# Tile-by-tile scaling at the norms of a two-block network, x ahead of the context in the odd norm, and the queries' rotation moved ahead of retention's gate projection

## What is computed

```python
def half_ffn(x, g, w1, w3, w2):
    return x + FFN_RES * swiglu(rmsnorm(x, g), w1, w3, w2)

def first_block(...):
    for layer in range(DEPTH):
        x = half_ffn(x, ...)
        h = rmsnorm(x, mix_norm[layer])
        x = x + (mixer_gla_rglru(h, ...) if layer % 2 == 0 else mixer_hgrn2(h, ...))
        x = half_ffn(x, ...)
        gate = jax.nn.sigmoid(rmsnorm(x, ple_norm[layer]) @ ple_gate[layer])
        x = x + gate * (p[layer] @ ple_proj[layer])
    return rmsnorm(x, final_norm)

def odd_layer(h, hc, w_in, w_out, q_norm, w_uq, kv_norm, w_ukv, decay_logit, need_ctx):
    cq, ckv, kr, rq, rk, rv, rg = split_cols(h @ w_in, widths)
    qn, qr, kn, vm = mla_up(cq, ckv)          # queries, keys, values from normed latents
    m = softmax_attention(qn, kn and knc, vm and vmc,
                          apply_axial_rope(qr, ang_r, ang_c), k_rope_all)
    r, r_c = retention_bidir(rq, rk, rv, ...)
    r = rms_norm(r) * jax.nn.silu(rg)
    return jnp.concatenate([m, r], axis=-1) @ w_out
```

## Time and profile before

| | before |
|---|---|
| median of 3 runs, us | 2898.67 |
| lowest and highest, us | 2896.55, 2899.17 |
| the profiled execution, us | 2900.66 |
| its span in the trace, us | 2898.5 |
| mean granted TensorE clock, share of full | 0.961 |
| TensorE matmul busy, share of the span | 90% |
| VectorE, ScalarE busy | 21%, 15% |

### The profile page before, as it was taken

How to read it: one execution, slowest core, us unless ns; L and a number is a source line. 1 busy time by engine, 2 the same in 40 slices (tenths; PEclk the granted TensorE clock), 3 DMA queues, 4 the chain that set the end, 5 groups by cost and what they waited for, 6 DMA issues and landing times.

```text
span 2898.5 us, 29860 instructions
## 1 busy us (share of the span) xinstructions
PE 2613.8 (90%) x12493; PEld 1816.4 (63%) x12493; DVE 618.5 (21%) x1323; ACT 442.3 (15%) x764; POOL 43.8 (2%) x55
## 2 busy tenths in 40 slices
PE   8999999999999999999999999898889998655656
PEld 7887788888888878888876563333334755211213
DVE  2011311022102241113134641211113143000002
ACT  1001310013002320003223520000002132000001
POOL 0000000000000011000000100000000000000000
PEclk9999999999999999999999999999999999788878
DMA  9446674455447487444422148999997216999997
GB/s 307 145 159 234 214 265 146 159 201 181 155 149 245 158 249 180 145 145 151 142 88 82 67 158 359 421 421 422 422 422 265 102 44 258 422 421 422 422 422 303
DMA packets 278241, 700.92 MB, mean 242 GB/s; under 512 B 16696, under 2 KB 200168, under 8 KB 230952
## 3 DMA queue, kind: packets, MB, share of 16 engines
q1 hardware_dynamic: 271088, 686.99, 63.8%
q10 hardware_dynamic: 4944, 8.07, 0.9%
q0 software_dynamic: 2112, 4.46, 0.8%
HBM read 695.30 MB, written 4.06 MB: 241 GB/s over the span
## 4 chain that ended last, share of the span: by engine, by line
PE 74%; DMA 19%; DVE 3%; issue 1%; SPq 1%; ACT 1%; ACTq 0%; DVEq 0%
PE bank L539 73%; DMA ring<-moe_w 19%; PE bank L548 2%; SPq L2952 1%; DVE AR L1571 0%; DVE AR L1574 0%; DVE AR L1583 0%; ACT AR L2386 0%; DVE H L1574 0%; DVE XC L1577 0%; DMA cst<-const 0%; DVE AR L1963 0%; ACT L2386 0%; DMA AR<-vec 0%; DVE H L1577 0%
## 5 line engine op out<-in xcount | busy, mean ns | idle before, releaser
L539 PE MATMUL bank<-H,ring 128*128 128x256 f32 (+1 forms) x5120 | 1149.2, 385 | 19.7 <-ACT H L2386 8.1
L539 PEld LDWEIGHTS bank<-H,ring 128*128 128x128 f32 (+1 forms) x5120 | 968.3, 190 | 188.5 <-issue 48.6
L539 PE MATMUL bank<-ring,AR 128*32 128x512 f32 (+1 forms) x2832 | 549.2, 703 | 204.0 <-DMA ring<-moe_w 196.7
L539 PEld LDWEIGHTS bank<-ring,AR 128*32 128x32 f32 (+1 forms) x2832 | 175.7, 140 | 559.6 <-issue 546.1
L539 PE MATMUL bank<-AR,ring 128*128 128x256 f32 (+2 forms) x1504 | 333.6, 380 | 5.1 <-DVE AR L1583 5.1
L539 PE MATMUL bank<-AR 128*128 128x256 f32 (+14 forms) x1200 | 307.0, 427 | 13.8 <-DVE AR L2289 6.2
L539 PEld LDWEIGHTS bank<-AR,ring 128*128 128x128 f32 (+2 forms) x1504 | 283.8, 189 | 47.9 <-DVE AR L1583 5.6
L2386 ACT ACTIVATE AR<-bank 128x512 f32<-128x512 f32 (+3 forms) x195 | 114.6, 590 | 1224.4 <-PE bank L539 816.2
L1571 DVE TENSOR_TENSOR AR<-bank,AR 128x512 f32<-128x512 f32 (+2 forms) x105 | 72.3, 689 | 832.2 <-PE bank L539 791.6
L539 PEld LDWEIGHTS bank<-AR 128*128 128x128 f32 (+7 forms) x1200 | 167.1, 181 | 113.5 <-issue 85.2
L2386 ACT ACTIVATE AR<-AR 128x512 f32<-128x512 f32 (+6 forms) x160 | 97.6, 635 | 866.9 <-DVE AR L1571 789.4
(11 more groups left out here) (124 smaller groups left out, 652.2 us busy)
## 6 DMA issues: line engine op xcount, KB each, us to landing
ring<-moe_w SPq DMA_DIRECT2D x368, 1024.0 KB, 15.5
ring<-ffn_w SPq DMA_DIRECT2D x132, 1024.0 KB, 5.2
ring<-ada_w SPq DMA_DIRECT2D x48, 1024.0 KB, 5.2
ring<-m_w_in SPq DMA_DIRECT2D x26, 1024.0 KB, 10.0
ring<-even_w_in SPq DMA_DIRECT2D x24, 1024.0 KB, 5.1
AR<-moe_w SPq DMA_DIRECT2D x18, 512.0 KB, 7.2
ring<-m_w_out SPq DMA_DIRECT2D x8, 1024.0 KB, 11.7
ring<-ple_gate SPq DMA_DIRECT2D x8, 1024.0 KB, 5.1
```

The source lines that it names most:

```text
L539: ins = pe.matmul(o, lhsT, rhs, start=start, stop=stop, skip_group_check=True)
```

## The change

1. **`y_full`** is raised by each of banks 0 to 3 as it fills, four times in a feed-forward, and VectorE waits for it bank by bank.
2. **`scaled_pair`**, a new function, scales two tiles. After feed-forwards 1 and 3 it stands behind each of the four additions; after ple of layer 0 likewise; after a mixer, pairs 0 and 1 stand behind additions 0 and 1, and pairs 2 and 3 behind the fourth (the out projection still reads those tiles of `H`). `feed_forward` and `ple` then begin with `presum`.
3. **The odd norm** does the eight tiles of x and then the eight of the context, on VectorE and ScalarE; each raises its semaphore. `cq` waits for the x tiles one by one, `ckv` for those of the context.
4. **The order of the odd layer**: `rg` moves from ahead of `qm` to behind `qr`, into banks 7 and 0; `kn` takes banks 1 to 7 and 0 once each, `vm` banks 4 to 7, and the wait for `vm` moves to the first output of the attention. ScalarE's copies and SP's loads follow.

```diff
@@ feed-forward, TensorE
-                               y_full if end and m == KT - 1 else None)
+                               y_full if end and m % 2 == 1 else None)
@@ attention, TensorE
                         else:
+                            if seq == "mla" and pair == 0:
+                                for t in range(4):
+                                    emptied(pe, f"vm{t}")
@@ odd, TensorE
-                                pe.wait_ge(h_ready, H_AT["odd"] - 2 * KT + 2 * k + 1)
+                                pe.wait_ge(h_ready, H_AT["odd"] - 2 * KT + k + 1)
...
-                    pe.wait_ge(h_ready, H_AT["odd"])
                     w = chunk(KT, 160)
                     b = fill("ckv", 1)
                     for k in range(KT):
+                        pe.wait_ge(h_ready, H_AT["odd"] - KT + k + 1)
...
                     tokens("rv1.", [2, 3], 4)
-                    features("rg0", [4], S)
-                    features("rg1", [5], S)
...
+                    features("rg0", [7], S)
+                    features("rg1", [0], S)
                     w = chunk(1, D)[:, 0, :].rearrange("p (h a) -> p h a", a=P)
                     for h in range(8):
-                        b = fill(f"kn.{h}", (7, 0, 1, 2)[h % 4])
+                        b = fill(f"kn.{h}", (h + 1) % 8)
...
-                        b = fill(f"vm{t}", (3, 4, 5, 6)[t])
+                        b = fill(f"vm{t}", 4 + t)
...
-                    for t in range(4):
-                        emptied(pe, f"vm{t}")
...
-                    idle_products(7)
+                    idle_products(0)
@@ VectorE
+            def scaled_pair(n, after, gains, g0):
+                dve.wait_ge(x_ready, 2 + 2 * (n // 2) if after == "init" else X_AT[after] - 3 + n)
+                for k in (2 * n, 2 * n + 1):
+                    ts(H[:, k, 0:S], XC[:, k, 0:S], column(gains, g0 + k), ALU.mult).then_inc(h_ready, 1)
@@ feed_forward, VectorE
-                dve.wait_ge(y_full, f + 1)
                 for b in range(4):
+                    dve.wait_ge(y_full, 4 * f + b + 1)
                     xs = XC[:, 2 * b:2 * b + 2, 0:S]
                     stt(xs, halves(b), 0.5, xs, ALU.mult, ALU.add).then_inc(x_ready, 1)
+                    if f % 2:
+                        scaled_pair(b, f"ffn{f}", "ple_norm", f // 2 * 8)
@@ add_output, VectorE
                     tt(xs, halves(b), xs, ALU.add).then_inc(x_ready, 1)
+                    for n in ((0,), (1,), (), (2, 3))[c]:
+                        scaled_pair(n, name, "ffn_norm", 8 if name == "mix0" else 24)
@@ ple, VectorE
                     tt(xs, GT[:, c, :].rearrange("p (a b) -> p a b", b=S), xs, ALU.add).then_inc(x_ready, 1)
+                    if l == 0:
+                        scaled_pair(c, "ple0", "ffn_norm", 16)
@@ mod_norm, VectorE
-                    for k in range(KT):
-                        for s in range(streams):
-                            ins = stt(H[:, k, s * S:(s + 1) * S], XC[:, k, s * S:(s + 1) * S], CA[:, k, s:s + 1],
-                                      RSTD[:, s * S:(s + 1) * S], ALU.mult, ALU.mult)
-                        ins.then_inc(scaled, 1)
+                    for s in range(streams):
+                        for k in range(KT):
+                            stt(H[:, k, s * S:(s + 1) * S], XC[:, k, s * S:(s + 1) * S], CA[:, k, s:s + 1],
+                                RSTD[:, s * S:(s + 1) * S], ALU.mult, ALU.mult).then_inc(scaled, 1)
@@ odd, ScalarE
+                    for n in range(4):
+                        take(f"qm{n}", ...)
                     for n in range(2):
                         take(f"rg{n}", RG[:, 2 * n:2 * n + 2, :], ACT.Silu)
-                    for n in range(4):
-                        take(f"qm{n}", ...)
@@ SP
-                for at, n in (..., (1184, 256),
-                              (1440, 256), (1696, 256)):
+                for at, n in (..., (1184, 256)):
                     columns_of(w, at, n)
                 load(rows(T["mla_w_uq_2"]), 2, 768)
+                for at in (1440, 1696):
+                    columns_of(w, at)
                 load(rows(T["mla_w_ukv_2"]), 1, D)
```

More of the change, by code:

```diff
@@ L1639, in first_x @@
                                     halves(b, P)).then_inc(x_ready, 1)
+            def scaled_pair(n, after, gains, g0):
+                dve.wait_ge(x_ready, 2 + 2 * (n // 2) if after == "init" else X_AT[after] - 3 + n)
+                for k in (2 * n, 2 * n + 1):
+                    ts(H[:, k, 0:S], XC[:, k, 0:S], column(gains, g0 + k), ALU.mult).then_inc(h_ready, 1)
             def scaled_x(name, after, gains, g0):
-                for k in range(KT):
-                    if k % 4 == 0 and after == "init":
-                        first_x(k // 4)
-                        dve.wait_ge(x_ready, 2 + 2 * (k // 4))
-                    elif k % 2 == 0 and after != "init":
-                        dve.wait_ge(x_ready, X_AT[after] - 3 + k // 2)
-                    ts(H[:, k, 0:S], XC[:, k, 0:S], column(gains, g0 + k), ALU.mult).then_inc(h_ready, 1)
+                for n in range(4):
+                    if n % 2 == 0 and after == "init":
+                        first_x(n // 2)
+                    scaled_pair(n, after, gains, g0)
                 presum(name)
@@ L1679, in feed_forward @@
             def feed_forward(f, after):
-                scaled_x(f"ffn{f}", after, "ffn_norm", 8 * f)
+                if f:
+                    presum(f"ffn{f}")
+                else:
+                    scaled_x("ffn0", after, "ffn_norm", 0)
                 if f == 0:
@@ L1891, in ple @@
             def ple(l, after):
-                scaled_x(f"ple{l}", after, "ple_norm", 8 * l)
+                presum(f"ple{l}")
                 if l == 0:
@@ L2417, in add_shift @@
                 emptied(act, "mods")
-                for k in range(KT):
-                    act.wait_ge(scaled, base + k + 1)
-                    for s in range(streams):
+                for s in range(streams):
+                    for k in range(KT):
+                        act.wait_ge(scaled, base + KT * s + k + 1)
                         hs = H[:, k, s * S:(s + 1) * S]
@@ L2802, in odd @@
                     load_decay(3)
+                    for n in range(4):
+                        take(f"qm{n}", QM[0:96, 2 * n:2 * n + 2, :], view=lambda b: b[0:96, :].rearrange("p (a b) -> p a b", b=S))
                     for n in range(2):
                         take(f"rg{n}", RG[:, 2 * n:2 * n + 2, :], ACT.Silu)
-                    for n in range(4):
-                        take(f"qm{n}", QM[0:96, 2 * n:2 * n + 2, :], view=lambda b: b[0:96, :].rearrange("p (a b) -> p a b", b=S))
                     for h in range(1, 8, 2):
@@ L3035, in load_early @@
                         else:
-                            sp.wait_ge(scaled, 32)
+                            sp.wait_ge(scaled, 40)
                         for row in range(2):
```

5 lines of the change are left out of this document (2 added, 3 removed).

## The result

The changed kernel takes 2881.44 us (median of four, 2880.47 to 2882.75) against 2898.82 us for the kernel before (four, 2896.55 to 2899.17): a ratio of 0.9938, with a 95% interval of 0.9926 to 0.995. It is faster by 17.4 us, where 20.8 were forecast. The profiled executions, 2878.3 and 2898.5 us of span, are 20.2 apart. First the page of the changed kernel: its span and the chain by line.

A forecast was written before the change was run, and what follows sets the result against it. TensorE's products one behind another bound the kernel (73% of the chain), expert weights 19%. Gains 1.47 + 3.35 + 1.86 + 4.75 + 0.5 + 8.9 = 20.8 us gave 2877.9 us; forecast 2874 to 2881, 8-in-10 range 2871 to 2885.

The forecast's parts named there:

- The four seams of block 1: Into feed-forwards 1, 2, 3 and layer 1's ple: earlier scalings nearly end TensorE's waits, gaining 1.47, 3.35, 1.86, 4.75 us.
- the slow products behind the waits: First 32 instructions behind the waits into feed-forward 2 and layer 1's ple: over pace by 1.76 and 1.75 us, counted as gain.
- The odd norm: Norm ahead of cq: ScalarE's first tile waits for one scaling, 0.40 us less, so cq starts earlier; gain taken as 0.5.
- the other end: Norm ahead of cq: no gain if the clock stays low to the same moment, or 2.3 us if it returns sooner.
- The rotation: Odd layer, up to the first scores: rg's projection covers the rotation, removing waits and slow instructions; gain 8.9 us, at least 7.5.
- the tie: First scores: ScalarE's table load ends about 2323.9, first exponential due about 2324.0; losing it leaves a gain of 7.5.
- 5.8 us of it are to spare; without it 5.1 us and the clock would be back: Odd layer: of rg's 13.8 us cover 5.8 are spare; without cover kn's 5.1 us wait and the low clock return.
- The streams shift with it, one for one: Both moe stages: transfers wait for slots TensorE frees, so the whole 20.8 us gained passes to the end.
- The first rival: Smaller leftovers: thin terms at ple, the transfers, odd norm and exponentials fail, 5.0 us less gain, 2883 us; chance 0.13.
- the transfers caught no tile: Mixer 1 to feed-forward 3: the rival had GpSimd's transfers hold up two scaled tiles, costing up to 1.3 us.
- The slower case: New seams and odd layer: several short waits keep the clock low, costing up to 50 us, 2928 us; chance 0.04.
- The signs named for a right forecast: Seam idle at most 0.6 us, 36 us from rv's end to first scores, mean clock above 0.961, moe stages same length.

The follow-up runs named there:

- pool_late: The kernel before, with GpSimd's na_rpb transfers started only when feed-forward 3's eight scalings are done: 2896.26 us against 2899.20, ratio 0.9988.
- odd_only: The kernel before with only the odd layer's new order, block 1 and the odd norm as before: 2891.04 us against 2898.45, ratio 0.9976.
- banks_only: The kernel before with rg where it was, kn spread over eight banks and vm in 7, 0, 1, 2: 2894.84 us against 2898.45, ratio 0.9989.
- half_cover: The changed kernel with rg0 back ahead of qm, only rg1 (32 instructions) behind qr: 2882.44 us, ratio 0.9942 to the kernel before.
- seams_filled: The kernel before with three waits filled by products of ones (ahead of feed-forward 2, ple of layer 1, fifth kn head): 2897.74 us against 2898.11.
- fill_both: The changed kernel with products of ones in two waits, 18 ahead of cq and 15 ahead of the second router: 2876.74 us against 2898.39, ratio 0.9925.

## Why the prediction was right, and where it was not

**The four seams of block 1** were right in mechanism and size. Forecast 1.47, 3.35, 1.86 and 4.75 (11.4 together); between the two traces 1.2, 3.5, 1.8 and 4.8, by the table's columns (11.3). The details came out too: a column of ple's seam took 1.97 us (649.18 to 651.15) where 2.0 were worked out, and 0.38 us were left of it (32 instructions in 652.10 to 659.39), where 0.5 were expected; feed-forward 3's additions came every 1.25 us for an expected 1.3, and nothing was left, for 0.1. One slip had no effect: at mixer 0 TensorE feeds an addition every 16 instructions, not "every 32 instructions or so"; the 3.45 us beside it is right (additions at 377.45, 380.90 and 384.36).

**The term that was mis-sized** is the slow products behind the waits: 1.76 at ple's seam and 1.75 at feed-forward 3's. I took them from one execution as if each had them, and that one, at 2900.66 us, was longer than all four that were timed (2896.55 to 2899.17). Of the four traces with the old seams unfilled, *ple0* has them in two and *ffn3* in three (pool_late: 9.6 behind the same wait). odd_only has at ple's seam

```profile
655.39 7.14 PE L539 MATMUL bank<-H,ring 128*128 128x256 f32 x32 [1.93 <-DVE H L1576]
```

where the earlier trace rows has 8.83 behind the same 1.93 us. Weighted so, the two seams are worth 2.6 and 4.4, which is 1.1 less than the 3.35 and 4.75 forecast. The even layer's second loss, 1.8 us in six of nine traces with the new seams, is 1.2 on average. Both are estimates from one trace per kernel.

**The odd norm**: forecast 0.5, measured 0.40 in the wait, as worked out, and 0.1 in *norm*. I had named the other end, "nothing, if the clock stays low to the same moment", and that is the nearer one. With the clock held up the same 128 instructions take 41.8.

**The rotation**: forecast 8.9, measured 8.7. ScalarE's table load and the first exponential came as close as worked out:

```profile
2309.59 1.28 ACT L2401 ACT_TABLE_LOAD   x1
...
2310.97 0.69 ACT L2401 ACTIVATE AR<-bank,AR 128x512 f32<-128x512 f32 x1
...
2316.18 2.97 PE L539 MATMUL bank<-AR 128*64 128x256 f32 x10 [0.25 <-ACT AR L2401]
```

The load ends 1.96 us behind the first scores (2308.91) and the exponential starts 2.06 behind them, where 2323.9 and 2324.0 behind 2321.94 were expected: the tie was not lost. The wait of 0.25 us further on is 0.10 in the traces with the old order. The size was right, part of the reason was not. The step "5.8 us of it are to spare; without it 5.1 us and the clock would be back" fails: without any cover, the eight banks bring 5.0 of the 8.7 (banks_only), since `kn` then waits for the first of a pair's three rotation steps and not for copies behind all twelve, and with them half the cover, 6.9 us where 8.0 would have been needed, leaves no wait (half_cover). I had seen that each bank is filled once and not worked out what that alone does.

**"The streams shift with it, one for one"** held for the first expert stage (*even* 899.1 and 898.9) and for the second (*experts* 447.0 and 447.1). It failed ahead of the second: *router* and *ranks* are 0.8 and 0.6 longer. I had looked for waits that the change removes and not at the one of 3.57 us that stays, behind which the clock now falls earlier (2.6 us behind TensorE's last product instead of 4.3). In the three traces with slow `kn` products (*odd* 73.8 to 74.0) *router* is 9.1, in all others without fillers there it is 9.9, seams_filled among them, whose order is the old one. So it isn't the new order as such. What ties the two places together stays open; the runs show only that they go together.

**The sum**: 20.8 less 1.1 for the seams' clock, 1.2 for the even layer, 1.4 ahead of the experts, 0.4 for the odd norm and 0.2 for the rotation is 16.5, against 17.4 measured with an interval of some 3.5 to either side. Odd layer alone and seams alone give 7.4 + 9.5 = 16.9 by medians. The first rival (smaller leftovers, 2883) came nearer to the median than the forecast of 2877.9 did, but by luck: of its four losses only the odd norm's came, while ple's seam kept the clock in all nine traces with the new seams, the transfers caught no tile and the exponentials' tie was not lost. The slower case did not occur: no new seam is followed by slow instructions. The signs named for a right forecast came: no idle over 0.6 us at the seams, 36.11 us up to the first scores, a mean granted clock of 0.964.

## What to carry to other kernels

Count the clock's part of a wait as a chance and not as a sum: a seam's price is the wait, plus the slow instructions times the share of executions that have them, and some of that can come back elsewhere. Behind a long wait that can't be removed, products on constants that end just inside it held the clock here, and two such places were worth 4.7 us by the medians, more than a new order of the odd norm. When an engine waits for copies behind another engine's long sequence, ask first whether a bank that is already free would do, before moving work under the sequence.

## What the runs showed of the hardware

Behind waits of the same length the clock fell in some traces and stayed up in others. Behind the same 1.93 us it fell in two traces and stayed up in two, behind 2.93 us it stayed up once in four, behind 3.05 us it fell in eight of fourteen, behind two waits of 0.89 and 0.66 us in seven of fourteen, and behind the 3.57 us ahead of the router it fell 4.3 us after TensorE's last product in the trace of before and 2.6 us in that of the changed kernel. Once it had fallen, a product of two instructions took 0.85 us instead of 0.43 (eight starts from 2422.88 to 2425.86 in the router of before).

With products of ones by ones in the wait the clock stayed at 2.4 GHz: in the window of fill_both over the fillers and the start of `cq` PEclk is 1.00, where the kernel before had 0.50 from its start of `cq` on the earlier trace rows.

```profile
2194.00:2199.00 5.00, 4.92 (x39) 4.36 (x38) 1.38 (x4) 4.28 (x6) 0.00 (x0) 1.00 1.08 363
```

Beside a transfer that GpSimd issues, VectorE's scalings were held, but not from the transfer's first moment. In the four traces with the old order and early transfers, those that started 0.28 and 0.33 us behind a transfer's start took 1.96 to 2.00 us, and those that started 0.02 to 0.07 us behind it 0.33 to 0.35 us; in the nine with the new seams the last scaling, 0.06 to 0.07 us behind, took 0.34 to 0.35 us. Additions of two tiles in SBUF kept their pace beside the same transfers: three of 128 x 512 from 1061.06 on in the changed kernel took 0.68 to 0.69 us each.
